# Projection tiles in passes of 512 and 64 columns in place of 288 and 288

## What is computed

```python
q, k, v, iq, ik, iw, za, cu, zc, gt = jnp.split(x @ w_in, cuts, axis=-1)   # 2048 -> 10832 columns
ga, gb = jnp.split(cu, 2, axis=-1)
u = ga * jax.nn.sigmoid(gb)                 # input of the causal convolution
...
a_br = (attn * jax.nn.silu(za)) @ w_att_out
c_br = (jax.nn.silu(layer_norm(c, ln_conv_g, ln_conv_b)) * jax.nn.silu(zc)) @ w_conv_out
gate = jax.nn.sigmoid(gt.astype(jnp.float32)).astype(x.dtype)
mixed = gate[..., 0, :] * a_br + gate[..., 1, :] * c_br
return layer_norm(DEEPNORM_ALPHA * x + mixed @ w_o, ln_post_g, ln_post_b)
```

## Time and profile before

| | |
|---|---|
| time, median of 3 runs | 1650.2 us (1648.29 to 1650.77) |
| the profiled execution | 1649.13 us, its span 1647.3 us |
| TensorE products | 1610.5 us busy (98%), 10897 instructions |
| TensorE weight loads | 1506.1 us busy (91%), 10897 instructions |
| VectorE, ScalarE, GpSimd | 682.4, 415.5 and 609.5 us busy |
| DMA | 173.00 MB, mean 105 GB/s |

### The profile page before, as it was taken

How to read it: one execution, slowest core, us unless ns; L and a number is a source line. 1 busy time by engine, 2 the same in 40 slices (tenths; PEclk the granted TensorE clock), 3 DMA queues, 4 the chain that set the end, 5 groups by cost and what they waited for, 6 DMA issues and landing times.

```text
span 1647.3 us, 27921 instructions
## 1 busy us (share of the span) xinstructions
PE 1610.5 (98%) x10897; PEld 1506.1 (91%) x10897; DVE 682.4 (41%) x1639; ACT 415.5 (25%) x507; POOL 609.5 (37%) x182
## 2 busy tenths in 40 slices
PE   8999999999999999999999999999999999999995
PEld 6888489999999989999999999999999999988884
DVE  4012977541122101217777777708472222111018
ACT  4222621242232211221111112222452111231120
POOL 4244033332322233344444444664343433433340
PEclk9999999999999999999999999999999999999998
DMA  6333133332233443622232332333345435532213
GB/s 248 87 102 89 36 95 81 98 99 74 72 93 107 135 125 115 195 78 78 78 92 64 94 86 77 78 87 92 98 133 154 134 106 158 182 137 98 80 51 115
DMA packets 245289, 173.00 MB, mean 105 GB/s; under 512 B 9771, under 2 KB 222219, under 8 KB 244347
## 3 DMA queue, kind: packets, MB, share of 16 engines
q1 hardware_dynamic: 240587, 162.20, 34.5%
q10 hardware_dynamic: 4608, 9.44, 1.5%
HBM read 155.70 MB, written 16.63 MB: 105 GB/s over the span
## 4 chain that ended last, share of the span: by engine, by line
PE 92%; DVE 3%; issue 1%; SPq 1%; DMA 1%; ACT 1%; POOL 0%; POOLq 0%; DVEq 0%; ACTq 0%
PE ps L1511 70%; PE ps L1498 11%; PE ps L1554 2%; PE ps L1694 1%; PE ps L1703 1%; PE ps L1495 1%; PE ps L1566 1%; PE ps L1494 1%; PE ps L1843 1%; DVE y L1458 1%; DVE y L1464 1%; SPq L498 1%; PE ps L1645 1%; PE ps L1668 1%; DVE bias L1165 1%
## 5 line engine op out<-in xcount | busy, mean ns | idle before, releaser
L683 POOL TENSOR_TENSOR wlo<-raw,whi 128x2048 fp32r<-128x2048 f32 x115 | 531.1, 4618 | 877.9 <-ACT whi L774 877.9
L1511 PE MATMUL ps<-xhi,whi 128*128 128x288 f32 (+2 forms) x2912 | 649.1, 300 | 3.2 <-ACT tmp_tanh L964 2.2
L1511 PE MATMUL ps<-xlo,whi 128*128 128x288 f32 (+2 forms) x2912 | 647.0, 300 | 0.0
L1511 PE MATMUL ps<-xhi,wlo 128*128 128x288 f32 (+2 forms) x2912 | 642.9, 298 | 0.0
L1511 PEld LDWEIGHTS ps<-xhi,whi 128*128 128x128 f32 x2912 | 471.6, 188 | 8.3 <-ACT tmp_tanh L964 2.4
L1511 PEld LDWEIGHTS ps<-xhi,wlo 128*128 128x128 f32 x2912 | 472.3, 188 | 3.0
L1511 PEld LDWEIGHTS ps<-xlo,whi 128*128 128x128 f32 x2912 | 471.9, 188 | 2.9
L774 ACT ACTIVATE whi<-raw 128x2048 fp32r<-128x2048 f32 x115 | 219.5, 1908 | 170.7 <-PE ps L1495 120.9
L1498 PE MATMUL ps<-whi,mixed 128*128 128x512 f32 x512 | 158.1, 390 | 0.5 <-POOL wlo L763 0.5
L1498 PEld LDWEIGHTS ps<-whi,mixed 128*128 128x128 f32 x512 | 95.8, 188 | 22.3 <-POOL wlo L763 1.8
L1349 DVE SCALAR_TENSOR_TENSOR ps<-U,dwT,ps 128x256 f32<-128x256 f32 x232 | 113.2, 488 | 0.0
(11 more groups left out here) (270 smaller groups left out, 1135.2 us busy)
## 6 DMA issues: line engine op xcount, KB each, us to landing
raw<-in_w_in_dram SPq DMA_DIRECT2D x83, 1024.0 KB, 5.7
raw<-in_w_o_dram SPq DMA_DIRECT2D x16, 1024.0 KB, 5.1
both_gates<-gates_dram SPq DMA_DIRECT2D x16, 576.0 KB, 6.9
raw<-in_w_att_out_dram SPq DMA_DIRECT2D x16, 512.0 KB, 4.2
raw<-in_w_conv_out_dram SPq DMA_DIRECT2D x16, 512.0 KB, 5.6
gates_dram<-tmp_gate ACTq DMA_DIRECT2D x24, 288.0 KB, 2.1
vpage<-in_cache_v_dram SPq DMA_DIRECT2D x32, 128.0 KB, 2.1
kTs<-in_cache_k_dram SPq DMA_DIRECT2D x32, 128.0 KB, 2.2
```

The source lines that it names most:

```text
L683: nc.gpsimd.tensor_tensor(wlo[:, buf, 0:width], raw[:, buf, 0:width], whi[:, buf, 0:width].bitcast(F32), ALU.subtract).then_inc(lo_ready, 1)
L1511: ins = mm(ps[:, bank + half, 0:width], w[b][:, k, :], x[:, k, t0 + half * width:t0 + (half + 1) * width], start=(k == k0 and m == 0), sto ...
```

## The change

The 512 columns from the first token of a tile on are one pass, the rest a second: 512 + 64 for 576 tokens, 512 + 80 for 592. The output is addressed through the flat view `ps_t`, and since 512 columns fill a bank, the results of a tile lie without a hole in two banks, and the readers take them as one row of 576 or 592. `take_u` reads the 528 prompt tokens in one instruction. The index-query tiles keep their one pass of 464. Weights, order and waits stay.

```diff
-            def tile_ps(b, width=OUTH):
-                return ps[:, 2 * b:2 * b + 2, 0:width]
+            def tile_ps(b, width=OUTW):
+                return ps_t[:, 1024 * b:1024 * b + width]
...
                 row = U[:, j, :]
-                nc.scalar.activation(row[:, TAIL:TAIL + HALF], ps[:, 2 * b, 0:HALF], ACT.Copy, scale=0.5)
-                nc.scalar.activation(row[:, TAIL + HALF:EXT], ps[:, 2 * b + 1, 0:LP - HALF], ACT.Copy, scale=0.5)
+                nc.scalar.activation(row[:, TAIL:EXT], tile_ps(b, LP), ACT.Copy, scale=0.5)
...
-                    gv = g[:, j, :].rearrange("p (h t) -> p h t", h=2)
-                    ins = nc.vector.scalar_tensor_tensor(gv, gv, 1.0, ps[:, o + 2 * c:o + 2 * c + 2, 0:OUTH],
-                                                         ALU.add, ALU.mult)
+                    gv, at0 = g[:, j, :], 512 * (o + 2 * c)
+                    ins = nc.vector.scalar_tensor_tensor(gv, gv, 1.0, ps_t[:, at0:at0 + OUTW], ALU.add, ALU.mult)
...
-            def tile_block(buf, bank, k0=0, kn=KC, t0=META, width=OUTH, each=None):
+            def tile_block(buf, bank, k0=0, kn=KC, t0=META, each=None):
...
-                        for half in range((TOK - t0) // width):
-                            ins = mm(ps[:, bank + half, 0:width], w[b][:, k, :],
-                                     x[:, k, t0 + half * width:t0 + (half + 1) * width],
+
+                        for c in range(t0, TOK, 512):
+                            out = 512 * bank + c - t0
+                            ins = mm(ps_t[:, out:out + min(512, TOK - c)], w[b][:, k, :], x[:, k, c:min(c + 512, TOK)],
                                      start=(k == k0 and m == 0), stop=(k == k0 + kn - 1 and m == 2))
...
-                    for half in range(2):
-                        ins = mm(ps[:, 4 + 2 * (k // 8) + half, 0:OUTH], b[:, 1, k * P:(k + 1) * P],
-                                 x[:, k, META + half * OUTH:META + (half + 1) * OUTH],
+                    for c in range(META, TOK, 512):
+                        out = 512 * (4 + 2 * (k // 8)) + c - META
+                        ins = mm(ps_t[:, out:out + min(512, TOK - c)], b[:, 1, k * P:(k + 1) * P],
+                                 x[:, k, c:min(c + 512, TOK)],
```

More of the change, by code:

```diff
@@ L782, in flat @@
             def flat(a, j, cols=OUTT):
-                return pairs(a[:, j, cols]) if isinstance(j, int) else \
-                    a[:, ds(j, 1), cols].rearrange("p a (h t) -> p (a h) t", h=2)
+                return a[:, j, cols] if isinstance(j, int) else a[:, ds(j, 1), cols].rearrange("p a t -> p (a t)")
             def each_pair(n0, count, take):
@@ L892, in take_gate @@
                     act.wait_ge(gate_stored[b], i * 16)
-                nc.scalar.activation(pairs(tmp_gate[:, b, :]), tile_ps(b), ACT.Tanh, scale=0.5).then_inc(tile_taken, 1)
+                nc.scalar.activation(tmp_gate[:, b, :], tile_ps(b), ACT.Tanh, scale=0.5).then_inc(tile_taken, 1)
                 act.wait_ge(tile_taken, N_GT - C_OF + b + 3 + i * 2)
@@ L970, in take_ga @@
                 row = U[:, j, :]
-                nc.scalar.activation(row[:, TAIL:TAIL + HALF], ps[:, 2 * b, 0:HALF], ACT.Copy, scale=0.5)
-                nc.scalar.activation(row[:, TAIL + HALF:EXT], ps[:, 2 * b + 1, 0:LP - HALF], ACT.Copy, scale=0.5)
+                nc.scalar.activation(row[:, TAIL:EXT], tile_ps(b, LP), ACT.Copy, scale=0.5)
                 nc.scalar.activation(sample_cols(U, j)[:, :, TAIL:],
-                                     ps[:, 2 * b + 1, LP - HALF:HALF].rearrange("p (b t) -> p b t", b=DB),
+                                     tile_ps(b, TOK)[:, LP:].rearrange("p (b t) -> p b t", b=DB),
                                      ACT.Copy, scale=0.5).then_inc(tile_taken, 1)
             def take_gb(j, b):
-                nc.scalar.activation(pairs(zc[:, j, :]), tile_ps(b, HALF), ACT.Tanh, scale=0.5).then_inc(tile_taken, 1)
+                nc.scalar.activation(zc[:, j, :], tile_ps(b, TOK), ACT.Tanh, scale=0.5).then_inc(tile_taken, 1)
             def take_zc(j, b):
@@ L1523, in one_tile @@
                 if isinstance(n0, int) and N_CU <= n < N_G2 and kind_at(n)[0] in ("ga", "gb"):
-                    cols = dict(t0=0, width=HALF)
+                    cols = dict(t0=0)
                 tile_block(n % 2, 2 * b, **cols).then_inc(block_used, 1)
@@ L1574, in _ @@
             ins.then_inc(dw_out, 1)
-            tile_pair(N_IQ, 0, t0=IQ0, width=IQW)
+            tile_pair(N_IQ, 0, t0=IQ0)
             pe.wait_ge(ikiwT_ready, 1)
@@ L1581, in _ @@
             ins.then_inc(ikiw_out, 1)
-            tiles(N_IQ + 2, 6, t0=IQ0, width=IQW)
+            tiles(N_IQ + 2, 6, t0=IQ0)
             pe.wait_ge(tile_taken, 8 + 2)
```

## The result

The changed kernel takes 1973.55 us (median of 4 runs, 1969.42 to 1974.07) against 1650.02 us before: ratio 1.1957, 95% interval 1.1936 to 1.1978. The profiled execution took 1974.07 us, its span 1972.3. The forecast of 1965 us, slower, holds within its range.

What follows compares the result with a forecast made beforehand. TensorE, busy 98%, was taken as the bound; 1649.1 + 265.4 (576-column tiles) + 52.8 (592-column tiles) - 2 (shorter waits) = 1965.3, so 1965 us, 19% slower; range 1940 to 2012 us, over 8 in 10.

Steps and rivals of the forecast that it cites:

- What bounds the kernel: Whole kernel: TensorE, busy 98% of 1647.3 us, sets the time, mostly in the projection passes of L1511, 70% of the span.
- what a short pass costs: Projection tiles: the next long pass's weight load shows during the short pass, which costs 112 ns, bounds 110 and 120.
- The long pass: Projection tiles: a pass of 512 columns was taken to cost 230 ns.
- the extrapolation of the 464-column row: Long pass estimated from 464-column passes with the same moving operand: 210.8 + 48 x 0.444 = 232.1 ns.
- the 342 taken: Projection tiles: ns for one pair of long and short pass, bounds 336.7 and 352.1.
- the 2 us that were taken: Waits inside the changed region, about 4 us, could shrink by 0 to 4; -2 us was taken.
- ScalarE's merged read: L971 and L972: two reads become one of about 650 ns, eight times; 1 us in all, hidden.
- (a): Projection pairs: the load stays hidden or isn't waited for, pair 263 ns, kernel 1634 us; chance 4%.
- The Trainium skill's spacing of short passes: Projection pairs: about 60 cycles for 1 to 64 columns, 518 for 512; pair 241 ns, some 108 us won.
- (b): Projection pairs: the load is cheaper than its record, short pass 64 ns, pair 294, kernel 1765 us; chance 4%.
- (c): Projection pairs: granted clock falls to 1.2 GHz now and then, 81 us per tenth of pairs, kernel 2046 us; chance 3%.

Runs made afterwards that it cites:

- e6: The changed kernel with each short pass made twice: 2478.01 and 2744.25 us.
- e9: The same kernel as e6, run once more to watch the granted clock: median 2477.29 us, 2436.45 to 2480.74.
- e7: The changed kernel with 64 of the 128 weight columns in the long passes (all but the first and last of each accumulation): 1756.45 us.
- e8: The changed kernel with 64 of the 128 weight columns in the short passes only: 1964.28 us.
- e1: The changed kernel's layout and readers with the old widths, 288 + 288 (288 + 304 for 592 tokens): 1647.33 us, ratio 0.9985 to before.
- e2: The changed kernel with passes cut 448 + 128 (448 + 144 for 592 tokens): 1852.11 us, ratio 1.1225 to before.
- e3: The changed kernel with passes cut 384 + 192 (384 + 208 for 592 tokens): 1731.16 us, ratio 1.0492 to before.
- e10: The changed kernel with each short pass made three times: 3338.54 us, ratio 2.0243.
- e5: Against e1, only the 16 tiles of 592 tokens cut 512 + 80, all others 288 + 288: 1702.01 us, ratio 1.0333 to before.

## Why the prediction was right

**What bounds the kernel** and **what a short pass costs** hold as written: e6 and e9 measure 110.8 to 111.6 ns for a pass of 64 columns, 112 was taken from L1727's loads; e7 and e8 show that it is the load for the next long pass. That only one is ahead at a time, which the prediction had read from 0.07 us between two loads of 80 columns, the loads at 1600 us show directly: the load for the next long pass starts 0.35 us after the one before, when the short pass begins, though a long pass of 0.23 us had room for 0.12 us more beside the load that it hides.

**The long pass** is the term that was mis-sized. I took 230 ns between the 512-column rows and the extrapolation of the 464-column row. The pair measures 343.9 ns, which with 110.8 to 111.6 ns for the short pass leaves 232.3 to 233.1, and that extrapolation had said 232.1. With the same moving operand and the same line it was the nearer row. A pair 1.9 ns over the 342 taken, by 4224 pairs, is 8 us, against a miss of 9.

**The rest** nearly cancels, and in part by luck. By the paces the pairs add (343.9 - 265.2) x 3.456 + (343.0 - 273.2) x 0.768 = 325.6 us. From the first tile of queries to the first pass of the output projection, the trace of before has 1233.41 + 190.40 - 214.70 = 1209.1 us, that of after 1748.68 - 218.44 = 1530.2: 321.1 more, 4.5 less than the pairs add. TensorE's idle time in these stretches fell from 4.3 to 2.1 us, the 2 us that were taken; the wait for `tmp_tanh` of 2.2 us is no longer in the list. The remaining 2.3 us were not foreseen: 17 tiles with attention steps behind them take 16.40 to 16.43 us each and not 48 x 343.9 ns = 16.51, which by this estimate is 1.5 us. It fits that their last short pass has no load for a long pass of the same tile behind it, but no run shows that apart. Ahead of all this the indexer, which the change leaves alone, took 4.4 us more: from the end of the last index-query tile to the first query tile 218.44 - 159.58 = 58.86 us, before 214.70 - 160.19 = 54.51. That is luck of the execution and not the change: e1, with the old widths, has 58.85 us there at a mean granted clock of 0.85, e8 54.51 us at 0.94. The window of after beside the earlier trace rows:

```profile
160.00:213.00 53.00, 47.33 (x175) 26.06 (x175) 42.37 (x136) 29.61 (x62) 0.00 (x0) 0.84 0.11 29
```

**ScalarE's merged read** was worth nothing on the path, as said; e1's small gain can't be put down to it by these runs.

**The rivals.** (a), the load hidden: out by the changed kernel and by e2 and e3, for which it would have meant no loss. It needed a short pass of at most 36.7 ns; the short pass costs three times that. The Trainium skill's spacing of short passes (TensorE: Matmul & The Clock Gate, section Back-to-back issue gap) would have made the kernel faster; the page gives it for isolated passes, with no time for their loads. The same page's section LDWEIGHTS gives a load as its columns over 1.2 GHz, 107 ns for 128. The runs come near it, with 110.8 to 111.6 ns for each short pass added. (b), the cheaper load: out, 111 and not 64 ns. (c), the clock: not in this kernel, whose tiles ran at 1.00 throughout with columns streaming in 240 of 344 ns. But with more short passes it fell: at two for each long pass in five of six executions, by their mean clocks, and at three for over 900 us. Its price was too low, as I let the load keep its 107 ns: with the 213 ns that the load takes at the low clock (below) it is an estimate of 422 x (427 + 213 - 344) ns = 125 us for each tenth of the pairs, and not 81.

## What to carry to other kernels

Where every pass loads its own weights, a pass costs the larger of its stream and the next load: here 0.444 ns a column and 5 ns, against 112 ns for 128 weight columns, so passes of 240 columns or more are full value, and a wide tile is best shared so that no pass falls under that. These figures are for 128 weight columns at the granted clock of 2.4 GHz and for the operands of this kernel. Filling a PSUM bank to its last column is worth nothing if it leaves a narrow remainder. To find the price before a change, look for any narrow pass in the trace and take the distance between its loads, not the duration of one.

## What was not expected of the hardware

- The granted clock fell to half for 82 us in e6, at the same place in e9, and for 102 and 819 us in e10. In three of these four stretches TensorE was not idle before it fell: 20 attention passes of 64 columns (2.7 us) stood there. The 819 us began behind 1.46 us of idle time, and then lasted through 16 tiles without any. The mix of passes does not decide alone, since most tiles in the profiled executions of e6, e9 and e10 ran at 1.00 with the same groups.
- A low mean clock is not confined to these kernels: of 73 executions of the kernel before, the changed one and e1 to e5, e7 and e8, three had one (two of the kernel before and one of e1, given with the result). They were not profiled, so what stood before the fall there is not known. Against that stand five of six (e6, e9) and two of two (e10). More short passes made the fall likelier; what decides it these runs don't show.
- The load slows with the clock: by an estimate from e10 it takes (1067 - 427)/3 = 213 ns at half, 427 ns being 512 columns at 1.2 GHz, against 111 at full.
- A load beside a long pass is not quite free: in e8, with 64 in place of 128 weight columns for the hidden load, the steady pair is 246.21/720 = 342.0 ns and not 343.9. (The short pass of e8 also writes only 64 partitions.) That the load takes the long pass's time is argued only; it would fit that 288 columns take 132.6 ns where 2.4 GHz needs 120.
